# A second block's mixers on one core: moved latent norm, rotated score slots, earlier splits, a shorter inverse root, and low parts summed by a transfer

## The reference

```python
for l in range(DEPTH):                                  # 2 layers
    h = rmsnorm(x, norm1_g[l])
    z = h @ w_in[l]                                     # 1024 x 6616 columns
    z_mla, z_nsa, z_fox, z_dsa, z_gate = split_cols(
        z, [MLA_COLS, NSA_COLS, FOX_COLS, DSA_COLS, GATE_COLS])
    o_mla = mla_mixer(...)     # c_q, c_kv = latents of 256 and 128 columns, each normed, then projected
    o_nsa = nsa_mixer(...)     # compressed, selected and window attention with a sigmoid gate
    o_fox = fox_mixer(...)     # causal attention with a forget gate
    o_dsa = dsa_mixer(...)     # indexer: 8 heads of relu(qi @ ki), top 64 keys, then attention
    lifted = einsum('bsnc,ncd->bsnd', branches, w_branch[l])
    gates = sigmoid(z_gate.reshape(B, S, 4, D_MODEL))   # 4096 of the columns of z
    x = x + sum(gates * lifted, axis=2) @ w_out[l]
    h2 = rmsnorm(x, norm2_g[l])
    x = x + square(relu(h2 @ w_up[l])) @ w_down[l]
```

## Time and profile before

| | |
|---|---|
| median of 3 runs | 1681.21 us (1676.3 to 1685.93) |
| the profiled execution | 1678.43 us |
| its span | 1676.7 us |
| mean granted TensorE clock | 0.968 |
| busy: PE, DVE, ACT, POOL | 92%, 49%, 44%, 35% of the span |
| transfers | 327 MB, 195 GB/s in the mean, all by SP's queue but the code loads |
| first layer's gate chunks | PE works on them from 789.5 to some 940 us |
| second layer's | from 1256.1 to some 1408 us |

### The profile page before, as it was taken

One profiled execution on the slowest core, in us unless ns is written; L12 is line 12 of the kernel. 1 busy time (PEld: TensorE's weight loads), 2 busy tenths in 40 slices (PEclk: granted clock), 3 DMA queues, 4 the chain that ended last, 5 costly groups with the idle time before them and its releaser, 6 DMA issues.

```text
span 1676.7 us, 23289 instructions
## 1 busy us (share of the span) xinstructions
PE 1550.4 (92%) x9590; PEld 1253.5 (75%) x9590; DVE 821.7 (49%) x1470; ACT 739.6 (44%) x1057; POOL 595.2 (35%) x227
## 2 busy tenths in 40 slices
PE   5999989999997999989889899999998798899997
PEld 4867867875996778578666658999886676589996
DVE  2734578324866764163664463522437733645222
ACT  3334366423436654143445344444434454354442
POOL 1200034320000442135555225655546443246543
PEclk9999889999997999999999999999999899999999
DMA  9597279769625786753343354555443333355550
GB/s 386 196 327 277 87 269 343 267 234 388 264 83 201 254 322 226 279 195 132 106 136 122 103 192 156 196 179 181 169 148 114 116 105 134 132 187 196 192 185 25
DMA packets 51225, 327.22 MB, mean 195 GB/s; under 512 B 5936, under 2 KB 5936, under 8 KB 17456
## 3 DMA queue, kind: packets, MB, share of 16 engines
q1 hardware_dynamic: 51120, 325.73, 53.8%
HBM read 324.66 MB, written 1.05 MB: 194 GB/s over the span
## 4 chain that ended last, share of the span: by engine, by line
PE 75%; DVE 17%; ACT 4%; DMA 2%; issue 1%; POOL 1%; DVEq 0%; SPq 0%; ACTq 0%
PE ps L224 19%; PE ps L225 18%; PE ps L226 18%; PE ps L221 16%; DVE lo L232 4%; DMA raw<-in_wmod 2%; DVE pb L2755 1%; PE ps L2704 1%; ACT hi L229 1%; DVE z L232 1%; DVE s L240 1%; ACT pb L229 1%; POOL lo L232 1%; DVE pb L232 1%; DVE rt L232 1%
## 5 line engine op out<-in xcount | busy, mean ns | idle before, releaser
L232 POOL TENSOR_TENSOR lo<-raw,hi 128x2048 fp32r<-128x2048 f32 (+2 forms) x76 | 354.2, 4670 | 647.4 <-ACT hi L229 647.4
L229 ACT ACTIVATE hi<-raw 128x2048 fp32r<-128x2048 f32 (+2 forms) x192 | 350.5, 1858 | 43.5 <-POOL big L232 16.9
L232 DVE TENSOR_TENSOR lo<-raw,hi 128x2048 fp32r<-128x2048 f32 (+1 forms) x116 | 291.8, 2531 | 97.1 <-ACT hi L229 96.9
L232 POOL TENSOR_TENSOR loh<-rawh,hih 128x1024 fp32r<-128x1024 f32 x64 | 156.0, 2450 | 141.9 <-ACT hih L229 141.6
L224 PE MATMUL ps<-hTh,hi 128*128 128x256 f32 x640 | 182.6, 285 | 5.4 <-DVE hTl L232 2.9
L225 PE MATMUL ps<-hTl,hi 128*128 128x256 f32 x640 | 181.8, 284 | 0.0
L226 PE MATMUL ps<-hTh,lo 128*128 128x256 f32 x640 | 181.7, 284 | 0.0
L224 PEld LDWEIGHTS ps<-hTh,hi 128*128 128x128 f32 x640 | 123.4, 193 | 7.2 <-issue 3.5
L224 PE MATMUL ps<-hi,hTh 128*128 128x512 f32 (+3 forms) x320 | 118.9, 372 | 10.2 <-DVE hTl L232 5.6
L225 PEld LDWEIGHTS ps<-hTl,hi 128*128 128x128 f32 x640 | 123.5, 193 | 0.5
L226 PEld LDWEIGHTS ps<-hTh,lo 128*128 128x128 f32 x640 | 123.5, 193 | 0.0
(11 more groups left out here) (306 smaller groups left out, 2990.1 us busy)
## 6 DMA issues: line engine op xcount, KB each, us to landing
raw<-in_wgu SPq DMA_DIRECT2D x64, 1024.0 KB, 4.9
raw<-in_wmod SPq DMA_DIRECT2D x48, 1024.0 KB, 6.9
raw<-in_wdn SPq DMA_DIRECT2D x32, 1024.0 KB, 5.6
rawh<-in_wgt SPq DMA_DIRECT2D x64, 512.0 KB, 3.8
raw<-in_wup SPq DMA_DIRECT2D x32, 1024.0 KB, 4.8
raw<-in_wdown SPq DMA_DIRECT2D x32, 1024.0 KB, 5.1
raw<-in_wz SPq DMA_DIRECT2D x12, 1024.0 KB, 4.7
raw<-in_wbr SPq DMA_DIRECT2D x8, 1024.0 KB, 4.9
```

Source lines behind the costliest of these rows:

```text
L229: return self.e.activation(o, a, f, **kw)
L232: return self.e.tensor_tensor(o, a, b, op)
```

## The change

1. **Adding transfer.** Of the four half chunks of each gate group, the second and fourth get their low part in another way. ACT rounds raw into hi and then writes -raw, rounded, over raw. POOL then issues a transfer from HBM with an add, which reads the chunk once more and adds it, so that raw - hi stands in the slot. This is 32 of the 64 gate chunks, 16 in each layer. The scratch for POOL's descriptors goes from 256 to 1024 bytes of a partition.
2. **Splits three ahead** for gate chunks, on ACT, DVE and POOL, where two were.
3. **Score slots by turns.** The n-th head of the indexer has slot n % 4, and its relu waits for head n - 4.
4. **Latent norm early.** The first part of `v_latent` stands in `v_indexer`, before its first yield, with `s1` as its scratch; the second stays in its place.
5. **Shorter inverse root.** `v_rstd` has 8 instructions with a scale, 7 without. ACT scales by 1/32 before squaring, and `v_stats` adds EPS in its one instruction, so it has 8 in all.

```diff
@@ source
-        return part(t_in["wgt"][at[0], at[1]], at[2], 1024), "pool"
+        return part(t_in["wgt"][at[0], at[1]], at[2], 1024), "dma" if at[2] % 2 else "pool"
@@ a_split
-            a.ac(c.hi, c.raw).then_inc(*a.up("hi"))
+            m = a.ac(c.hi, c.raw)
+            if c.how == "dma":
+                m = a.ac(c.lo, c.raw, scale=-1.0)
+            m.then_inc(*a.up("hi"))
@@ g_split
+            elif c.how == "dma":
+                g.wait_ge(*g.at("hi", c.key))
+                g.e.dma_start(c.lo, c.src, accum_op=ALU.add).then_inc(*g.up(f"low{c.r}", 16))
                 g.mark("lo", c.key)
@@ v_rstd
+        scale, *c = self.ROOT
+        if inv_n is not None:
+            v.ts(ss, ss, inv_n, EPS, ALU.mult, ALU.add).then_inc(*v.up("dve"))
+        v.ts(dst.bitcast(I32), ss.bitcast(I32), -0.5, 1597463007.0, ALU.mult, ALU.add).then_inc(*v.up("dve"))
+        v.stt(tmp, dst, scale, dst, ALU.mult, ALU.mult).then_inc(*v.up("dve"))
         v.tt(tmp, tmp, ss, ALU.mult).then_inc(*v.up("dve"))
...
+        v.stt(ss, tmp, c[0], tmp, ALU.add, ALU.mult).then_inc(*v.up("dve"))
+        for x in c[1:3]:
+            v.stt(ss, ss, x, tmp, ALU.add, ALU.mult).then_inc(*v.up("dve"))
+        v.stt(dst, ss, c[3], dst, ALU.add, ALU.mult).then_inc(*v.up("dve"))
@@ v_stats
-        v.tt(ss, ss, self.st[:, c0 + 2:c0 + 4], ALU.add).then_inc(*v.up("dve"))
+        v.stt(ss, ss, EPS, self.st[:, c0 + 2:c0 + 4], ALU.add, ALU.add).then_inc(*v.up("dve"))
@@ a_fill, v_fill, g_fill
-                self.a_split(a, "gt", l, g, i, ahead=2)
+                self.a_split(a, "gt", l, g, i, ahead=3)
@@ a_indexer
-                        h = 4 * i + 2 * j2 + j
-                        if n % 2:
-                            a.wait_ge(*a.at("idx head", l, n - 1))
-                        elif n >= 8:
-                            a.wait_ge(*a.at("idx head", l, n - 7))
-                        a.ac(self.s2[:, 256 * (h % 4):256 * (h % 4) + nk], ps[:, b, 256 * i:256 * i + nk], ACT.Relu,
+                        if n >= 4:
+                            a.wait_ge(*a.at("idx head", l, n - 4))
+                        a.ac(self.s2[:, 256 * (n % 4):256 * (n % 4) + nk], ps[:, b, 256 * i:256 * i + nk], ACT.Relu,
@@ v_indexer
         v.ts(V.wi, self.z[:, :, SM + 16:SM + 24], 8 ** -0.5, None, ALU.mult).then_inc(*v.up("dve"))
+        self.v_latent_in(v, l)
         yield
@@ kernel
-        nc = bacc.Bacc("TRN2", target_bir_lowering=False, num_devices=1, dynamic_dma_scratch_size=256)
+        nc = bacc.Bacc("TRN2", target_bir_lowering=False, num_devices=1, dynamic_dma_scratch_size=1024)
```

More of the change, by code:

```diff
@@ L46 @@
 SMALL = ("sil", "cst", "col", "x", "cx", "row", "pos", "gb00", "gb01", "gb10", "gb11", "fg")
+SEMS.update({f"low{r}": f"a chunk's low part is summed in half slot {r}" for r in range(NR, NR + 2 * RMIX)})
 SEMS.update({f"in_{k}": f"{k} landed" for k in SMALL})
@@ L536, in g_split @@
                 g.tt(c.lo, c.raw, c.hi.bitcast(F32), ALU.subtract).then_inc(*g.up("lo_pool"))
+                g.mark("lo", c.key)
+            elif c.how == "dma":
+                g.wait_ge(*g.at("hi", c.key))
+                g.e.dma_start(c.lo, c.src, accum_op=ALU.add).then_inc(*g.up(f"low{c.r}", 16))
                 g.mark("lo", c.key)
@@ L657, in v_rstd @@
         v.wait_ge(*v.last)
-        v.stt(dst, tmp, 1.5, dst, ALU.add, ALU.mult).then_inc(*v.up("dve"))
-        c = 0.375 ** 0.5
+        v.stt(ss, tmp, c[0], tmp, ALU.add, ALU.mult).then_inc(*v.up("dve"))
+        for x in c[1:3]:
+            v.wait_ge(*v.last)
+            v.stt(ss, ss, x, tmp, ALU.add, ALU.mult).then_inc(*v.up("dve"))
         v.wait_ge(*v.last)
[L661 to L667, removed]
+        v.stt(dst, ss, c[3], dst, ALU.add, ALU.mult).then_inc(*v.up("dve"))
     def a_stats(self, a, name, src, ready, buf, c0, *freed, halves=(0, 1)):
@@ L676, in a_stats @@
                     a.wait_ge(*a.last)
-                a.ac(buf[:, 0:512], src[:, t, 512 * h:512 * h + 512], ACT.Square,
+                a.ac(buf[:, 0:512], src[:, t, 512 * h:512 * h + 512], ACT.Square, scale=1.0 / 32,
                      accum_out=self.st[:, c0 + 2 * h + t:c0 + 2 * h + t + 1]).then_inc(*a.up("act"))
@@ L1801, in a_moe @@
                     a.wait_ge(*a.last)
-                a.ac(self.s1[:, 0:512], self.x[:, t, 512 * h:512 * h + 512], ACT.Square,
+                a.ac(self.s1[:, 0:512], self.x[:, t, 512 * h:512 * h + 512], ACT.Square, scale=1.0 / 32,
                      accum_out=self.st[:, 2 * h + t:2 * h + t + 1]).then_inc(*a.up("act"))
@@ L2291, in v_fill @@
             for i in range(4):
-                self.v_split(v, "gt", l, g, i, ahead=2)
+                self.v_split(v, "gt", l, g, i, ahead=3)
                 yield
@@ L2331, in g_fill @@
             for i in range(4):
-                self.g_split(g, "gt", l, gg, i, ahead=2)
+                self.g_split(g, "gt", l, gg, i, ahead=3)
                 yield
@@ L2903, in v_latent @@
         self.v_rope(v, self.z[:, :, ML + 384:ML + 416].unsqueeze(2), 16, 0)
+    def v_latent(self, v, l):
+        V, ps = self.views2(), self.ps
         yield
```

24 lines of the change are left out of this document (10 added, 14 removed).

## The result

The changed kernel is slower: 1684.07 us (median of 10 runs, 1679.48 to 1688.63) against 1676.15 us for the kernel before beside it (10 runs, 1674.36 to 1685.93). The ratio is 1.0042, with a 95% interval from 1.0028 to 1.0057, so some 7 us more. I had forecast 21 us less. The profiled execution took 1681.72 us with a span of 1679.9; that is 3.3 us more than before.

The account below looks back on a forecast made before the run. PE was taken as the bound, idling mostly for DVE in the gate stretches. Terms of -9.4 and -10.3 us for two layers and -1.6 made -21.3, so 1657, and 1660 us as run median; range 1647 to 1688.

Parts of the forecast that it names:

- Adding transfer: Odd gate chunks: low part lands in 6.5 us; short cover costs +2.4 us a layer, net 0 at the second chunk.
- Splits three ahead: Gate chunks: earlier roundings remove the later PE wait for POOL's `loh`, -1.1 us in each layer.
- Latent norm early: Latents' turn: PE's waits go whole because the norm runs in DVE's earlier idle time, -3.7 and -4.1 us.
- Slots by turns: Indexer, each layer: -2.5 us at compressed probabilities and POOL's wait before; -1.6 at `big` and the scores' maximum.
- Forget mixer: Its DVE scaling no longer runs beside a POOL subtraction, now a transfer: -1.4 of a 2.3 us PE wait.
- ACT: Gate stretches: ACT's added instructions sometimes stand in front of an exponential and delay PE, +1 us a layer.
- The clock: Gate stretches: shorter waits win back a third of the time lost to the lowered clock, -2.5 and -3 us.
- Roots: Inverse roots at the end, before block one's odd layer and elsewhere: fewer DVE instructions, -1.6 us in all.
- A: Rival, odd gate chunks: transfer takes 10 to 12 us from issue to landing, PE waits, 1690 us; chance 0.20.
- B: Rival, gate stretches: DVE stays the bound and removed waits return at its next result, 1676 us; chance 0.20.
- C: Rival, gate chunks: landing as a plain load's 3.8 plus 1 us issue, cover holds entirely, 1650 us; chance 0.12.
- The rule that I weighed under the adding transfer: POOL's transfer descriptors use ports that DVE's two-port modes lock; an issue would be late by 0.2 to 0.7 us.

Follow-up runs that it names:

- e9: Kernel before with only the early latent norm, slots by turns and shorter inverse root; POOL subtracts everywhere, splits two ahead: ratio 0.9942.
- e1: Changed kernel, but POOL subtracts every gate chunk's low part again, with no adding transfers: ratio 0.9972 to the kernel before.
- e2: Changed kernel, but POOL's window sums wait for its last copy of the keys, not its own latest transfer: 1670.56 us, 0.9960 to the kernel before.
- e6: Kernel before with the indexer's slots by turns as the only change: ratio 1.0007.
- e14: e2 with the indexer's slots put back as in the kernel before: ratio 1.0040 to the kernel before.
- e13: Kernel before with only the early latent norm and the shorter inverse root: ratio 0.9942.
- e7: Kernel before with splits three ahead in place of two as the only change: ratio 1.0049.
- e12: e2 with plain transfers that overwrite the low part and add nothing, so the sum is left out: 1648.24 us, 0.9826 to the kernel before.
- e17: e2 with each gate chunk's eight high-part products ahead of its four low-part ones: 1656.93 us, 0.9873 to the kernel before.

## Why the prediction was wrong, step by step

Measured, the way from the kernel before to the changed one has four stairs:

| stair | ratio after it | step |
|---|---|---|
| latent norm, slots, roots (e9) | 0.9942 | -0.6% |
| splits three ahead (e1) | 0.9972 | +0.3% |
| adding transfers, without the own wait (e2) | 0.9960 | -0.1% |
| the wait for the own transfer (changed kernel) | 1.0042 | +0.8% |

The third step is within the noise, as the intervals of e1 and e2 overlap. Against the forecast of -21 us the result of +7 is 28 us off. By these stairs and 1676 us, the latent norm, slots and roots gave 9.7 us where I had 17.6; three ahead cost 5.0 where I had a gain of 2.2; the adding transfer without its wait gave 2.0 where I had 1.5 (+4.0, and -5.5 for the clock); and POOL's wait for it cost 13.7 where I had nothing. That the third agrees is luck. In e2 PE's waits for `loh` are 22.0 us in both layers together, not 9.4 (2.4, and 2.3 at the second chunk, in each), and the waits for DVE that e1 has and e2 has not paid for them.

**The step that failed** is "Adding transfer". It priced what PE waits for and left out what else waits for the transfer: I went through the chunks, but not through the `last` of POOL's own program, though a wait of the issuing engine is the first thing to look for when an instruction becomes a transfer. That one wait turned the sign of the result, and it is half of the miss. Without it the whole change would have been 0.9960, still 14 us short of the forecast.

The second failure is the size in the same step, "I take 6.5 from semaphore to landing". It was 7.7. From this came waits of 12.3 and 10.1 us against 2.4, and 2.3 at the second chunk. The second chunk's transfer took 9.4 us in the first layer, so PE waited 5.07 there:

```profile
793.80 0.66 PE L225 MATMUL ps<-hih,hTh 128*128 128x512 f32 x1 [5.07 <-DMA loh<-in_wgt]
794.26 0.63 PE L226 MATMUL ps<-loh,hTh 128*128 128x512 f32 x1
794.69 0.63 PE L227 MATMUL ps<-hih,hTl 128*128 128x512 f32 x1
```

Behind it the matmuls start 0.43 us apart where 0.23 is their pace at the full clock: the lower of the two levels.

**Splits three ahead** I had at -1.1 in each layer. Alone they cost 8 us in all. I asked what ACT would wait for, and not what the earlier subtractions would stand beside, though the collision that the prediction names first was that very thing.

**Latent norm early**, -3.7 and -4.1: right. It runs in DVE's idle time, with no collision, and PE's wait at the latents is gone:

```profile
795.77 0.56 DVE L233 TENSOR_TENSOR s<-z 128x384 f32<-128x384 f32 x1
...
798.50 0.38 DVE L238 TENSOR_SCALAR st<-st 128x4 f32<-128x4 f32 x2
```

Two instructions in 0.38 us where one took 2.30.

**Slots by turns**, -2.5 and -1.6: the rows are as foreseen. The relus run in fours:

```profile
808.64 1.21 ACT L230 ACTIVATE s<-ps 128x256 f32<-128x256 f32 x4 [0.37 <-PE ps L222]
```

The waits shrank by 3.3 and 1.7, but not by this alone: e6 shows 1.9 more instead for the first. The step priced DVE's sum at 0.54 us a head, as if POOL stood still, and did not ask what ACT's earlier roundings let POOL do beside it: 5.51 us for three heads. It takes the transfers to make the slots worth 0.8% (e14).

**Forget mixer**, -1.4: wrong. Its scaling took 2.33 us beside POOL, not 0.28, since a subtraction that stayed now falls on it, and PE waited 3.0 where it was 2.3. The earlier splits brought it there: with two ahead the wait is 2.3 (e9, e13), with three ahead alone 3.5 (e7).

```profile
922.32 2.33 DVE L237 TENSOR_SCALAR s<-z 128x256 f32<-128x256 f32 x1
```

**ACT**, +1.0: no wait of PE grew behind it. **The clock**, -2.5: it went to 0.92 and, by my estimate from 0.03 of 157 us, took some 5 us in each layer in place of giving any. I had made it follow the sum of the waits. It does so roughly: 0.99 with 12.4 us of waits over the first stage in e12, 0.92 with 22.7 here. But before has 0.95 with 19.6, e2 0.97 with 19.3 and e17 0.96 with 14.2, so the sum alone doesn't give it. **Roots**, -1.6: right in sign, 4.2 alone (0.9975, 2 to 6 us). What my count left out I have not taken apart.

Of the rivals, A named a right place and, by luck, the price, but not the way: landing took 7.7, under its 9 us, its 15 us of waits were not reached, and half of the miss is POOL's own wait, which A doesn't have. B's mechanism is that of e1. That e1 also shows B's -0.3% is chance, as B's sum holds 6.8 us for transfers that e1 doesn't make. In the changed kernel PE's waits for DVE are 5.8 us, under B's 12. C's landing of 4.8 was near e12's 5.5, which came out at 1648 where C had 1650; this too is partly luck, since C counted gains for slots and splits that e6 and e7 don't show alone. The rule that I weighed under the adding transfer, an issue late by one DVE instruction, shows in no issue: POOL's 16 issues take 0.87 to 1.01 us. Whether it is in the spread of the landings, 6.6 to 9.4, I have not taken apart.

## What to carry to other kernels

When work moves from an engine to a transfer, list every wait that names that engine's latest step, its own first: what was free in program order becomes a wait for a landing. Price a transfer by the cover of each user and not by the mean, and before making it faster ask whether its reader can want it later; here, beside adding transfers, the order of PE's products was worth more (0.9%) than any part of the change by itself. And a lead of one more step, or an engine set free sooner, is not free: look at what the earlier instructions will stand beside (e7 and e6, three subtractions in a row both times).

## What the runs showed of the hardware

- A transfer of 512 KB from HBM landed in 3.8 us when SP issued it, in 5.5 when POOL did and in 7.7 when it adds; 256 KB with an add in 5.8. POOL's issue takes 0.57 us plain and 0.88 with an add. The queues spent 1.8 times the share on 16.78 MB added as on 16.78 MB copied. The Trainium skill (DMA: Bandwidth & Descriptors, section SWDGE vs HWDGE vs iDMA) calls descriptors written by GpSimd slower to set up and more flexible; the trace agrees, by 1.4 us beside the plain loads of the same run (4.1).
- Three POOL subtractions in a row (7.1 to 7.3 us) held four short DVE instructions for 7.32 us (e7), and three longer ones for 5.51 where 1.56 was enough (e6).
- SP's own loads of gate chunks went from 3.8 to 4.7 us beside the adding transfers, and to 4.1 beside plain ones.
- One idle stretch of PE of 2.7 us was followed by the lower clock level, and the 64 small matmuls behind it took 3.49 us in place of 1.97. That wait cost 4.2 us at its place, not 2.7 (changed kernel and e2).
